# Turn tables, last squares, memory evacuations, a norm's root and a difference's norm placed elsewhere in a two-block transformer kernel

## The reference

```python
# block 1, each layer (layer 0: mixer_ab, layer 1: mixer_c)
h = h + rmsnorm(mix, gains[1])
ff = jnp.square(jax.nn.relu(rmsnorm(h, gains[2]) @ w_up)) @ w_down
h = h + rmsnorm(ff, gains[3])
h = h + jax.nn.sigmoid(h @ w_ple_gate) * (p @ w_ple)
# block 2, each layer
h = _rms_norm(x, attn_norm) @ w_in
o_d = _rms_norm(p(q1, k1) @ v - lam * (p(q2, k2) @ v), diff_sub_norm) * (1.0 - lam_init)   # difference group
q_e = _rms_norm(_heads(mem_q, 4), mem_q_norm)              # memory group: the queries' norm
mem_kv = _rms_norm(mem, mem_norm) @ mem_w_kv               # a projection of 256 memory tokens
o_e = softmax(q_e @ k_e.T / 8) @ v_e
x = x + concat(o_a, o_b, o_c, o_d, o_e) @ w_o
x = x + (silu(dwconv(_rms_norm(x, ffn_norm) @ w_gate)) * (xn @ w_up)) @ w_down
```

## Time and profile before

| | |
|---|---|
| median of 3 runs | 1517.23 us (1515.94 to 1520.54) |
| profiled execution | 1518.34 us, span 1517.0 us |
| mean granted clock of PE | 0.979 |
| PE busy | 96% of the span |
| DVE, ACT, POOL busy | 66%, 51%, 7% |
| moved by DMA | 228.19 MB, mean 150 GB/s |

### The profile page before, as it was taken

How to read it: one execution, slowest core, us unless ns; L and a number is a source line. 1 busy time by engine, 2 the same in 40 slices (tenths; PEclk the granted TensorE clock), 3 DMA queues, 4 the chain that set the end, 5 groups by cost and what they waited for, 6 DMA issues and landing times.

```text
span 1517.0 us, 26059 instructions
## 1 busy us (share of the span) xinstructions
PE 1451.9 (96%) x10884; PEld 1376.7 (91%) x10884; DVE 997.7 (66%) x1503; ACT 777.5 (51%) x1219; POOL 110.4 (7%) x100
## 2 busy tenths in 40 slices
PE   7999989999998889999999989999999998999999
PEld 7989979999986789999997779999998787899999
DVE  5575676654678657654486765877755676577763
ACT  6744445444474544444376665544445685543443
POOL 0014112100001001110000000011100000011100
PEclk9999989999999999999999988999999998999999
DMA  8532245555463236655544312556555421255553
GB/s 260 161 111 84 61 155 179 191 182 182 158 202 132 73 107 190 184 182 194 180 155 153 120 59 72 176 170 190 175 193 189 137 84 56 90 181 177 190 177 105
DMA packets 186573, 228.19 MB, mean 150 GB/s; under 512 B 5964, under 2 KB 161228, under 8 KB 186456
## 3 DMA queue, kind: packets, MB, share of 16 engines
q1 hardware_dynamic: 185448, 221.75, 45.7%
q0 software_dynamic: 1008, 4.77, 0.9%
HBM read 225.46 MB, written 1.05 MB: 149 GB/s over the span
## 4 chain that ended last, share of the span: by engine, by line
PE 70%; DVE 17%; ACT 8%; issue 3%; DMA 1%; POOL 0%; DVEq 0%; ACTq 0%; SPq 0%; POOLq 0%
PE bank L495 20%; PE bank L497 20%; PE bank L496 20%; DVE weights_low L786 6%; ACT weights_high L684 3%; PE bank L503 2%; PE bank L1002 2%; ACT S L2107 2%; PE bank L2052 2%; DVE cv L2910 1%; PE bank L2031 1%; DVE S L2182 1%; DVE cv L2907 1%; DVE pad L2897 1%; DMA weights_raw<-in_w_in_ab 1%
## 5 line engine op out<-in xcount | busy, mean ns | idle before, releaser
L786 DVE TENSOR_TENSOR weights_low<-weights_raw,weights_high 128x1024 fp32r<-128x1024 f32 (+2 forms) x421 | 507.2, 1226 | 289.4 <-ACT weights_high L684 289.2
L684 ACT CAST weights_high<-weights_raw 128x1024 fp32r<-128x1024 f32 (+2 forms) x421 | 424.7, 1031 | 257.1 <-PE bank L497 254.8
L495 PE MATMUL bank<-hT_high,weights_high 128*128 128x256 f32 x1640 | 472.1, 288 | 15.3 <-DVE hT_low L858 5.0
L496 PE MATMUL bank<-hT_low,weights_high 128*128 128x256 f32 x1640 | 467.6, 285 | 0.0
L497 PE MATMUL bank<-hT_high,weights_low 128*128 128x256 f32 x1640 | 467.6, 285 | 0.0
L495 PEld LDWEIGHTS bank<-hT_high,weights_high 128*128 128x128 f32 x1640 | 318.1, 194 | 20.9 <-issue 9.8
L496 PEld LDWEIGHTS bank<-hT_low,weights_high 128*128 128x128 f32 x1640 | 318.0, 194 | 0.3
L497 PEld LDWEIGHTS bank<-hT_high,weights_low 128*128 128x128 f32 x1640 | 317.7, 194 | 0.2
L495 PE MATMUL bank<-aT_high,weights_high 128*128 128x256 f32 x864 | 242.3, 280 | 0.2
L496 PE MATMUL bank<-aT_low,weights_high 128*128 128x256 f32 x864 | 241.2, 279 | 0.0
L497 PE MATMUL bank<-aT_high,weights_low 128*128 128x256 f32 x864 | 241.1, 279 | 0.0
(11 more groups left out here) (417 smaller groups left out, 1830.8 us busy)
## 6 DMA issues: line engine op xcount, KB each, us to landing
weights_raw<-in_w_up SPq DMA_DIRECT2D x32, 1024.0 KB, 5.4
weights_raw<-in_w_down SPq DMA_DIRECT2D x32, 1024.0 KB, 5.1
weights_raw<-in_ffn_w_gate SPq DMA_DIRECT2D x22, 1024.0 KB, 5.3
weights_raw<-in_ffn_w_up SPq DMA_DIRECT2D x22, 1024.0 KB, 5.3
weights_raw<-in_w_in SPq DMA_DIRECT2D x20, 1024.0 KB, 5.0
weights_raw<-in_w_in_ab SPq DMA_DIRECT2D x16, 1024.0 KB, 5.9
weights_raw<-in_ffn_w_down SPq DMA_DIRECT2D x16, 1024.0 KB, 5.5
weights_raw<-in_w_o SPq DMA_DIRECT2D x10, 1024.0 KB, 6.1
```

The source lines that it names most:

```text
L495: k.E.matmul(out, xh, wh, start=first, stop=False)
L496: k.E.matmul(out, xh, wl, start=False, stop=False)
L684: k.A.copy(w.halves(n)[0], w.raw_part(n)).then_inc(*k.s.weight_high(n))
L786: k.V.tensor_tensor(low, w.raw_part(n), high.bitcast(F32), ALU.subtract).then_inc(*k.s.weight_low(n))
```

## The change

The results are the same but for rounding; what changes is where things are issued.

- In ff1 and ff2 ACT squares the last quarter before it casts the next parts. In ff1 of layer 0 the angle tables (DVE) are made behind output pair 0 of the down phase, and their sines (ACT) behind pair 1.
- The sums of squares at the end of ff1 come three product groups into the gate projection of ple.
- In mixer c the last split of each token linear comes behind the evacuation of its results; the turning of the keys (`turned_heads(1024, ...)`) comes ahead of the memory's; the memory projection is one part ahead of before, its splits follow a written-out list, its evacuations to `kvm` come in `work(2)` and `work(4)`; all QK copies are ACT's.
- In m2 the memory queries are no longer divided by their root before the scores, the scores are multiplied by the inverse root (`query_factor`); the difference's norm comes behind the scores of group 5 (`behind_scores`); a split of the next weights comes ahead of the inverse of a norm (`meanwhile`); the outputs have two slots instead of one, and the last turning of an output comes amid the products of the one before.

```diff
--- before.py
+++ after.py
@@ -465,7 +465,7 @@
-        m.out = [v[:, 6:8, :] for v in k.hT]
+        m.out = [v[:, 4:8, :] for v in k.hT]
...
@@ -811,14 +811,18 @@
-def vector_token_linear(k, key, n0, evacuate=None, between=None):
+def vector_token_linear(k, key, n0, evacuate=None, between=None, evacuated_first=False):
     for k0 in (0, 4):
         n = k.w.first(key + (k0, n0))
         for i in range(2):
-            vector_split(k, n + i + 1)
-            if k0 + 2 * i == DC - 2 and evacuate is not None:
+            last = k0 + 2 * i == DC - 2 and evacuate is not None
+            if not (last and evacuated_first):
+                vector_split(k, n + i + 1)
+            if last:
                 for t in range(NT):
                     evacuate(t)
+            if last and evacuated_first:
+                vector_split(k, n + i + 1)
             if between is not None:
                 next(between, None)
...
@@ -1709,20 +1713,16 @@
         tensor_pair_panels(k, st, p, m.aT, DFF1 // P, ("down", layer), lambda c: s.active.at((st, c - c % 2)))
-    tensor_sums_by_token(k, (st, "post"))
 
 
 def scalar_feed_forward_1(k, layer):
     A, s, m, st = k.A, k.s, k.ff1[layer], ("ff1", layer)
-    if layer == 0:
-        for which in range(2):
-            A.wait_ge(*s.angles.at(which))
-            A.activation(k.trig_table[:, which, :, :], k.trig_table[:, which, :, :], ACT.Sin).then_inc(*s.trig(which))
     for n0 in range(0, DFF1, 256):
         c, i = n0 // P, n0 // 256 % 2
+        if c == 0:
+            scalar_last_squares(k, st)
         scalar_split(k, k.w.first(("up", layer, 0, n0)) + 2)
         if c == 0:
-            scalar_last_squares(k, st)
             scalar_sums_root(k, st, m.R)
...
@@ -1731,6 +1731,10 @@
         scalar_out_squares(k, st, p)
+        if layer == 0 and p == 1:
+            for which in range(2):
+                A.wait_ge(*s.angles.at(which))
+                A.activation(k.trig_table[:, which, :, :], k.trig_table[:, which, :, :], ACT.Sin).then_inc(*s.trig(which))
     scalar_sums_root(k, (st, "post"), m.post_inv)
...
@@ -1769,8 +1773,6 @@
-    if layer == 0:
-        vector_turn_tables(k)
...
@@ -1793,6 +1795,8 @@
         vector_out_gained(k, st, p, m.u, post_gain(k, layer, 1))
+        if layer == 0 and p == 0:
+            vector_turn_tables(k)
...
@@ -1820,8 +1824,11 @@
     def post_factor():
-        yield
-        yield
+        for _ in range(3):
+            yield
+        tensor_sums_by_token(k, (("ff1", layer), "post"))
+        for _ in range(3):
+            yield
         tensor_along_tokens(k, (("ff1", layer), "post"), k.ff1[layer].post_inv)
...
@@ -1919,33 +1926,41 @@
+MEMORY_SPLITS = (0, 0, 3, 3, 5, 5, 7)
...
 def tensor_memory_projected(k):
 
-    for l in range(2):
-        yield from tensor_token_parts(k, ("mem", l), ("mem_kv", l), k.mem.memT[l], 0, 512)
+    parts = itertools.chain(*[tensor_token_parts(k, ("mem", l), ("mem_kv", l), k.mem.memT[l], 0, 512) for l in range(2)])
+    next(parts)
+    for _ in parts:
+        yield
...
 def vector_memory_projected(k):
 
-    n, m = k.w.first(("mem_kv", 0, 0, 0)), k.mem
-    for part in range(8):
-        vector_split(k, n + part - part % 2)
-        if part % 4 == 3:
-            l = part // 4
-            k.V.wait_ge(*k.s.inverse.at("mem"))
-            for t in range(NT):
-                key = (("mem", l), 0, t)
-                k.V.wait_ge(*k.s.products.at(key))
-                k.V.tensor_scalar(k.kvm[l][:, t, :], k.banks[key][:, :], m.inv[:, t:t + 1], None, ALU.mult).then_inc(*k.banks.read(key))
-        yield
+    n = k.w.first(("mem_kv", 0, 0, 0))
+    for upto in MEMORY_SPLITS:
+        vector_split(k, n + upto)
+        yield
+
+
+def vector_memory_evacuated(k, l):
+
+    k.V.wait_ge(*k.s.inverse.at("mem"))
+    for t in range(NT):
+        key = (("mem", l), 0, t)
+        k.V.wait_ge(*k.s.products.at(key))
+        k.V.tensor_scalar(k.kvm[l][:, t, :], k.banks[key][:, :], k.mem.inv[:, t:t + 1], None, ALU.mult).then_inc(*k.banks.read(key))
...
@@ -2066,7 +2091,14 @@
-        tensor_deep_panel(k, st, held, a.out, 2 * (j % a.slots), a.key + (k0, 0), ready, j == 0, n == len(a.groups) - 1)
+        amid = last_turned() if n == len(a.groups) - 2 else iter(())
+        tensor_deep_panel(k, st, held, a.out, a.out_chunk(n), a.key + (k0, 0), ready, j == 0, n == len(a.groups) - 1, amid)
...
@@ -2079,7 +2111,7 @@
-    for c in range(0, g.blocks, 2 if a.copies_by_scalar else 4):
+    for c in range(0, g.blocks, 2):
...
@@ -2180,6 +2198,8 @@
+                elif g.query_factor is not None:
+                    op = V.tensor_tensor(dst, bank, spread(g.query_factor[:, t, own], 2, nk), ALU.mult)
...
@@ -2235,7 +2255,7 @@
-    skewed([(4, out_turned), (3, values), (2, turned), (0, amid), (1, scores), (4, out_products), (0, prepared), (0, next_ready)], len(a.groups))
+    skewed([(4, out_turned), (3, values), (2, turned), (0, amid), (1, scores), (1, behind_scores), (4, out_products), (0, prepared), (0, next_ready)], len(a.groups))
...
@@ -2336,16 +2357,18 @@
     projected(1024)
+    turned_heads(1024, 4, 1024)
     vector_memory_turned(k)
     projected(0)
-    turned_heads(1024, 4, 1024)
     turned_heads(0, 8, 0)
     projected(512)
...
     def work(n):
-        if n == 1:
+        if n in (2, 4):
+            vector_memory_evacuated(k, n // 2 - 1)
+        if n == 2:
             turned_heads(512, 8, 512)
...
@@ -2405,9 +2428,10 @@
-    return Attention(("m2", l), m, groups, 1, ("o_2", l), m.out, copies_by_scalar=True, late=(1,))
+    return Attention(("m2", l), m, groups, 2, ("o_2", l), m.out, copies_by_scalar=True, late=(1,))
...
@@ -2583,14 +2606,14 @@
-    def work(n):
-        if n == 5:
-            roots("memq", SLOT["memq"], 4)
-
     def finish(n):
         if n == 3:
+            roots("memq", SLOT["memq"], 4)
+
+    def behind_scores(n):
+        if n == 5:
             scalar_root(k, (st, "sub"), m.st2[:, :, 0:4])
...
@@ -2722,7 +2752,7 @@
-        scaled(DIFF)
+        scaled(DIFF, meanwhile=lambda: vector_split(k, n2 + 2))
...
@@ -2777,10 +2807,13 @@
         if n == 5:
             squared(MEMQ)
-            scaled(MEMQ)
+            V.wait_ge(*s.reduced.last())
+            V.tensor_scalar(queries, queries, 64 * EPS, None, ALU.add).then_inc(*s.mean((st, "memq")))
...
```

85 lines of the change are left out of this document (48 added, 37 removed).

## The result

The changed kernel took 1522.47 us in the median (1520.39 to 1525.63, 10 runs), the kernel before beside it 1517.99 us (1514.52 to 1520.77, 10 runs). The ratio is 1.0031 with a 95% interval of 1.002 to 1.0043: slower by 4.5 us, where 6.5 us less were forecast. The profiled execution of the change took 1525.63, with a span of 1524.3 and a mean granted clock of 0.968 (before 0.979).

A forecast was written before the change was run, and what follows sets the result against it. PE, busy 96%, was taken as the bound, so gains come only from its waits and low clock. Terms -6.0 - 0.2 - 0.5 + 3.0 - 2.0 - 0.8 = -6.5 gave 1510.7, predicted as 1511 us; range 1501 to 1520.

The forecast's parts named there:

- The start of ff1: Layer 0: moving the angle tables and squares removes a PE wait and low clock behind it, -6.0 us.
- that rival: Down phase of ff1: no room for the tables' 5.0 us on DVE, +4, total 1515; chance 0.17.
- Mixer c: Evacuations to kvm behind low parts hold banks and make PE wait, +3.0 us; bounds -0.6 and +10.2.
- the third new wait: Mixer c: group 2 waits for the values of group 0, about 2.4 us.
- the mixer of block 2: Steps (a) to (f) together: -1.0 us in each layer; bounds -3.9 and +1.5 per layer.
- (c): Block 2's mixer: scores of group 5 no longer wait 4.6 us for the difference's chain; exponentials begin at 917.5.
- (d): Block 2's mixer: the difference's root queues behind exponentials on ACT; of up to 7.6 us won, 0.5 are left.
- (f): Block 2's mixer: the wait of 4.6 us draws a low stretch of 6.8, +2.0 us.
- (b): Block 2's mixer: the memory queries' root leaves the path ahead of hT_low; PE goes on 3.4 us earlier.
- (e): Block 2's mixer, behind the difference: waits for group 5 and the last turning's wait go, -3.0 us.
- (a): Block 2's mixer: the split ahead of an inverse removes a wait of 2.68 us; chain only 1.6 us earlier.
- a held bank holds everything: Slower rival: mixer c's three waits each draw 6.8 us at half clock, +10.2, m2 +1 each; 1522, chance 0.18.

The follow-up runs named there:

- ff1, ple and ff2 alone: The kernel before with only the change's parts in ff1, ple and ff2: 1512.67 us, ratio 0.9959.
- a kernel of its own: The kernel before with only the change's parts in mixer c: 1525.03 us, ratio 1.0036.
- Filling the wait: The change with 36 transposes of a constant on PE in its wait for the difference, both mixers of block 2: 1514.5 us, ratio 0.9982 to the kernel before.
- the norm in front: The change with the difference's norm back ahead of the scores of group 5, sharing the queries' root's table load: 1507.5 us, ratio 0.9927 to the kernel before.
- the late split: The norm in front, with block 2's split n5+1 back behind the inverse of the norm: 1509.9 us, ratio 0.995 to the kernel before.
- the run with ff1 filled: The change with norm in front and evacuations to kvm ahead of low parts, plus 20 constant transposes ahead of ff1's first products: 1493.49 us, ratio 0.9841.

## Why the prediction was wrong

**Right.** The start of ff1 was forecast to take 15.6 us instead of 19.75, and did; ff1, ple and ff2 alone are faster by 6.2, where 7.5 were forecast for them together. The tables on DVE are hidden in the down phase, so that rival is out.

**Right in part by luck.** Mixer c was forecast at +3.0 with its mechanism, the held banks, and the two waits at 5.4 each; they were 4.72 and 3.69, and the stretch +2.6 in the change, +5.5 as a kernel of its own. But the terms of the sum were other ones. The waits that it names were to grow by 5.2 us; the third new wait, of 2.4, didn't come, and they grew by 0.4 (8.41 in place of 8.04). For the low clock it took -0.4; there were 20.6 us of it in place of 6.8 behind the two waits, and PE was busy 4.2 us longer in the stretch (123.29 against 119.11). Too much for the waits and too little for the clock met near the right number.

**The steps that failed** are in the mixer of block 2, forecast at -1.0 and measured at about +3 a layer: (c) with (d), by 2.9 us, and (f), by 2.7.

(c) and (d) had the exponentials of group 5 begin at 917.5 and the difference turned 0.5 us earlier than before. Counted from the first product of the mixer, which lies 0.8 later in the change (786.18 against 785.41), the exponentials began 4.7 us earlier than before instead of 7.6, and the difference was turned 2.4 us later (142.4 against 140.0). What (c) left out is a wait for ACT: the scores of group 5 are now multiplied by the memory queries' inverse root, and ACT makes this root behind its copies of PT and a table load. DVE in the change, right ahead of these scores:

```profile
917.34 0.20 DVE L805 RECIPROCAL st<-st 128x8 f32<-128x8 f32 x1 [2.44 <-ACT st L716]
```

So more than half of the 4.2 us that (c) counted for leaving out the difference's chain went into this wait; in (b), too, this place was reached 2.7 us earlier and not 3.4.

(f) said: "Against this the wait of 4.6 should draw a low stretch of 6.8, of which some 4 us hold products: +2.0." The wait was there, at 3.97, but it drew 10.4 us, and all of it held products. Filling the wait puts this at 4.7 us a layer by the stage times, 3.7 by the ratios, in place of 2.0. That m2 isn't off by the whole 5.6 has two reasons: up to 0.9 is the cut at the squares, and the end of the mixer gained somewhat more than (e) had.

In (a) the removed wait of 2.68 was followed by one of 2.04 at the exponentials, with 10.4 us at low clock behind it where before 3.4 lay behind the first. This loses nothing further on: with the norm in front the same wait had 3.4 us at low clock behind it, and PE still came to the scores of group 5 no sooner than in the change (129.6 and 128.9 us behind the mixer's first product). But it also gained little of what was counted: the late split can't tell the early one from none.

**What stood behind it.** The prediction compared the wait for the difference only with the kernel before: turned at 924.9 instead of 925.41. It didn't ask what the change would be with this one step left out. The norm in front measured that, 7.8 and 7.5 us. The chain of the norm needs ACT once. In front it shares the root's table with the memory queries' root, and its first steps fall into the 2.44 us in which DVE waits for that root; behind the scores it queues behind eight exponentials and a table load of its own:

```profile
921.22 0.51 ACT L2139 ACTIVATE S<-S,mx 128x256 f32<-128x256 f32 x1 [2.62 <-DVE mx L2210]
...
925.29 1.28 ACT L716 ACT_TABLE_LOAD   x1
```

(ACT's timeline of the change.)

**A smaller miss** may be the end of ff1, forecast at -0.5 in layer 1. The sums no longer make PE wait, but PE now waits twice for the next operand, in both layers alike. In layer 0 of the change, at the same place:

```profile
404.00 0.36 PE L495 MATMUL bank<-gate_hT_high,weights_high 128*128 128x256 f32 x1 [0.55 <-DVE gate_hT_low L860]
...
408.02 0.36 PE L495 MATMUL bank<-gate_hT_high,weights_high 128*128 128x256 f32 x1 [0.96 <-DVE gate_hT_low L860]
```

The two are 1.5 us together, where 0.90 was removed. Whether the end of ff1 gained or lost in sum isn't settled, as the traces without the change spread over 2.7 us in this stretch. The starts of ff2 gave nothing that shows. The time of the change, 1522.47, is that of the rival "a held bank holds everything" (1522), but not by its sum: it had c at +10.2, which cost a quarter of that in the trace, and m2 at +1 a layer, which cost about three times as much.

## What to carry to other kernels

Before a chain is moved behind other work, ask when its result is next needed and what each of its steps will queue behind on its new place: here a norm of 4 us on DVE was moved off work that had time, and its root landed behind eight exponentials, with PE waiting for it. An instruction that frees a bank and whose input is ready belongs ahead of one that waits for another engine; two such pairs of instructions were worth 10 us. A factor that moves from one place to another takes its wait with it: ask whether the engine that makes it will be done. And a wait that is new on PE is to be priced with the slow products behind it, if these end last, and compared with the kernel that has all other parts of the change, not only with the one before.

## What the runs showed of the hardware

- The low stretch behind a wait was 10.4 us at 1.2 GHz behind waits of 3.97 and 2.04 us, but 3.4 behind one of 2.01 and 6.8 behind one of 3.22 in the kernel before; the same wait of 2.04 had 3.4 us behind it with the norm in front: its length doesn't follow that of the wait.
- The clock also fell without a wait of 2.0 us or more, against what the rows of before showed: in layer 1 of the run with ff1 filled it was at 0.50 from 551 on, among waits of 1.30 and 0.64 us.
- Transposes of a constant, with no other purpose, kept the granted clock at 1.00 through a wait of 4 us and the 10 us behind it. They also bring it back: in layer 0 of the run with ff1 filled PE did nothing else from 203.60 to 206.6, and the clock rose from 0.50 to 1.00 in that time.
- What lies ahead of ff1 was the same in both kernels and took 204.56 and 207.35 us in the two profiled executions (204.34 to 207.41 in 12 traces): a profiled execution has to be compared stretch by stretch, not by its end.
